# Gate weights gathered into one 36-column block; the first attention scores issued masks first, even and odd heads in turn

## The reference, cut to what matters

```
h = rmsnorm(x, norm1_g[l]);  proj = h @ w_in[l]
mq, mk, mv, mo, mi, mf, aq, ak, av, su = split(proj)
# (1) mi, mf: the input and forget gates of the mLSTM, 4 heads each, 8 columns of w_in in all
# (2) softmax attention, 8 heads of 64 features, 256 tokens, one block, causal:
s_own = einsum('bhqd,bhkd->bhqk', q, k) * scale
s_own = where(kpos <= qpos, s_own, -inf);  p = softmax(s_own)
```

## Time and profile before

| | us |
|---|---|
| median of three runs | 1274.5 |
| lowest, highest | 1273.63, 1278.43 |
| the profiled execution, its own time | 1275.59 |
| its span on the core | 1273.8 |
| TensorE busy (matmuls) | 1070.6 |
| VectorE busy | 460.3 |
| ScalarE busy | 180.1 |
| GpSimd busy | 22.4 |
| mean granted TensorE clock | 0.922 of 2.4 GHz |

### The profile page before, as it was taken

The page is one execution under the profiler, slowest core; times in us unless marked ns, Lnnn a source line. Parts: engine busy times, 40 slices in busy tenths (PEclk is TensorE's granted clock), DMA queues, the critical chain, the costliest instruction groups (busy, mean ns, idle before and its releaser), DMA issues.

```text
span 1273.8 us, 22730 instructions
## 1 busy us (share of the span) xinstructions
PE 1070.6 (84%) x9476; PEld 578.6 (45%) x9476; DVE 460.3 (36%) x1253; ACT 180.1 (14%) x427; POOL 22.4 (2%) x34
## 2 busy tenths in 40 slices
PE   5999999999967777776799999899677777679977
PEld 4476655454533333333355755554333333334533
DVE  0786345433322222222247753533222222224331
ACT  2314310010100000000024161100000000000100
POOL 3000002000000000000000000000000000000000
PEclk9999999999988888888899999999888888889998
DMA  9711379999999999999993313899999999997996
GB/s 313 261 71 67 132 291 355 389 428 426 430 427 427 425 428 429 427 427 427 391 339 141 133 67 132 353 387 428 427 427 427 426 428 427 428 427 327 427 426 278
DMA packets 50660, 440.16 MB, mean 346 GB/s; under 512 B 9320, under 2 KB 12040, under 8 KB 25488
## 3 DMA queue, kind: packets, MB, share of 16 engines
q1 hardware_dynamic: 48672, 436.33, 83.1%
q0 software_dynamic: 800, 0.99, 0.5%
q10 hardware_dynamic: 1104, 1.59, 0.4%
HBM read 437.31 MB, written 1.05 MB: 344 GB/s over the span
## 4 chain that ended last, share of the span: by engine, by line
PE 55%; DMA 40%; DVE 2%; issue 1%; DVEq 1%; ACT 0%; ACTq 0%; SPq 0%
DMA ring<-in_e_w_up_dram 39%; PE PS L1468 12%; PE PS L1531 9%; PE PS L1505 7%; PE PS L1767 4%; PE PS L1430 4%; PE PS L1421 4%; PE PS L1525 3%; PE PS L1440 2%; PE PS L1701 1%; PE PS L1721 1%; PE PS L1481 1%; DMA gT<-in_norm_g_dram 1%; PE PS L1657 1%; PE PS L1824 1%
## 5 line engine op out<-in xcount | busy, mean ns | idle before, releaser
L1468 PE MATMUL PS<-ring,hT 128*32 128x256 f32 x4608 | 336.6, 452 | 164.1 <-DMA ring<-in_e_w_gate_dram 107.7
L1468 PEld LDWEIGHTS PS<-ring,hT 128*32 128x32 f32 x4608 | 181.8, 125 | 339.6 <-issue 275.9
L1505 PE MATMUL PS<-ring,hT 128*32 128x512 f32 x1152 | 134.2, 607 | 8.5 <-issue 8.2
L880 DVE TENSOR_SCALAR hT<-hT 128x256 f32<-128x256 f32 x36 | 11.0, 306 | 302.4 <-ACT hT L613 302.4
L1531 PE MATMUL PS<-ring,hT 128*128 128x512 f32 x256 | 114.8, 602 | 0.0
L1430 PE MATMUL PS<-cst,ring 64*64 64x64 f32 x1216 | 81.2, 282 | 5.8 <-ACT ring L608 1.4
L1430 PEld LDWEIGHTS PS<-cst,ring 64*64 64x64 f32 x1216 | 77.0, 212 | 15.1 <-issue 11.9
L887 DVE TENSOR_TENSOR hT<-hT,PS 128x256 f32<-128x256 f32 x36 | 15.2, 422 | 174.7 <-PE PS L1468 174.7
L1421 PE MATMUL PS<-xres,scr 128*64 128x512 f32 x304 | 73.6, 605 | 0.0
L1531 PEld LDWEIGHTS PS<-ring,hT 128*128 128x128 f32 x256 | 48.1, 193 | 54.7 <-issue 54.6
L608 ACT COPY ring<-PS 128x512 f32<-128x512 f32 x38 | 22.3, 587 | 352.6 <-PE PS L1421 352.6
(11 more groups left out here) (341 smaller groups left out, 901.9 us busy)
## 6 DMA issues: line engine op xcount, KB each, us to landing
ring<-in_e_w_gate_dram SPq DMA_DIRECT2D x64, 2048.0 KB, 41.2
ring<-in_e_w_up_dram SPq DMA_DIRECT2D x64, 2048.0 KB, 44.0
ring<-in_e_w_down_dram SPq DMA_DIRECT2D x60, 2048.0 KB, 42.7
ring<-in_w_in_dram SPq DMA_DIRECT2D x10, 2048.0 KB, 18.8
ring<-in_w_out_dram SPq DMA_DIRECT2D x2, 4096.0 KB, 13.1
ring<-in_e_w_down_dram SPq DMA_DIRECT2D x8, 1024.0 KB, 39.5
ring<-in_w_in_dram SPq DMA_DIRECT2D x2, 1024.0 KB, 23.3
xres<-in_x_dram ACTq DMA_DIRECT2D x1, 1024.0 KB, 8.7
```

The lines of the kernel that those rows point to most:

```text
L1468: last = pe.matmul(PS[o:o + UT, bank, 0:256], xTe[:, k, UT * u:UT * u + UT], w[u][:, k, :, 2 * h:2 * h + 2], start=k == 0, stop=k == KD - 1)
L1505: last = pe.matmul(PS[o:o + UT, 3, :], hTe[:, c % 2, hc:hc + UT], w[u][:, c, 512 * h:512 * h + 512], start=c == 0, stop=c == KF - 1)
```

## The change

It has two parts. Part one: GpSimd waits for chunk 0 of `w_in`, clears a new block `wgates` of 8 x 36 columns (in tile 8 behind the chunk), and copies the eight gate columns into it, four to columns 0 to 3 and four to columns 32 to 35; TensorE waits for that (`s_wg`) and makes the gates with one matmul of 36 weight columns per feature block. The clearing of `v65`, `bb` and `taps` stands behind this in GpSimd's list. Part two: the first row tile's scores are issued differently. First two bf16 matmuls write the masks of four heads each, over a whole bank; then the eight fp32 matmuls of heads 0 to 7 add to them, even and odd heads in turn.

```diff
+        wgates = tile(8, KD * 264, KD * (32 + MH)).rearrange("p (k n) -> p k n", k=KD)
...
+                pool.wait_ge(s_win[0], 32 * (l + 1))
+                pool.memset(wgates, 0.0)
+                pool.drain()
+                for g in range(2):
+                    last = pool.tensor_copy(wgates[:, :, 32 * g:32 * g + MH], wchunk(0)[:, :, 256 + MH * g:256 + MH * g + MH])
+                last.then_inc(s_wg, 1)
                 pool.memset(v65[:, :, :, HD], 1.0).then_inc(s_zr, 1)
...
+                pe.wait_ge(s_wg, l + 1)
                 for k in range(KD):
-                    for g in range(2):
-                        last = pe.matmul(PS[32 * g:32 * g + MH, 1, 0:T], wchunk(0)[:, k, 256 + MH * g:256 + MH * g + MH],
-                                         hT[:, k, :], start=k == 0, stop=k == KD - 1)
+                    last = pe.matmul(PS[0:32 + MH, 1, 0:T], wgates[:, k, :], hT[:, k, :], start=k == 0, stop=k == KD - 1)
...
-                    if u >= 2:
-                        pe.wait_ge(s_pr, 6 * l + (u - 1))
-                    else:
-                        pe.wait_ge(s_qT, 4 * l + 4)
+                    pe.wait_ge(s_pr, 6 * l + (u - 1))
...
-                scores(0)
-                scores(1)
+                def first_scores():
+
+                    pe.wait_ge(s_qT, 4 * l + 4)
+                    for u in range(2):
+                        pe.matmul(PS[:, 6 + u, :].rearrange("p (i k) -> p i k", k=P), one16,
+                                  mask.unsqueeze(1).broadcast_to([P, 4, P]), start=True, stop=False)
+                    for h in range(AH):
+                        r = slice(64 * (h % 2), 64 * (h % 2) + 64)
+                        last = pe.matmul(PS[:, 6 + h % 2, P * (h // 2):P * (h // 2) + P], qkT[r, 0, h // 2, 0:P],
+                                         qkT[r, 1, h // 2, 0:P], start=False, stop=h >= AH - 2)
+                        if h >= AH - 2:
+                            last.then_inc(s_as, 1)
+
+                first_scores()
                 vo_part(0)
```

More of the change, by code:

```diff
@@ L220, in build @@
         s_wo = sem("w_out_in")
+        s_wg = sem("gate_columns_spread")
         s_tile = [sem(f"expert_tile_in_{t}") for t in range(NTILE)]
```

## The result

The changed kernel takes 1284.24 us, the median of 20 runs (1278.91 to 1289.72); the kernel before takes 1276.41 us beside it (20 runs). The ratio is 1.0055, with a 95% interval of 1.004 to 1.0069: slower by 7 us by the ratio, by 7.8 us between the two medians. I had forecast 1275.5 (1272 to 1280).

A forecast was written before the change was run, and what follows sets the result against it. TensorE's list was first suspect in the mixers, with VectorE the other parent at turn_probs(0). 1275.6 less 1.25 (1.07 scores, 0.18 gates) gives 1274.3; one clock fall (1.64) 1276.0, less 0.5 for the base: 1275.5 us, range 1272 to 1280.

The forecast's parts named there:

- The scores' work: First row tile's scores in each layer: 1.6 us (1.4 to 2.9) instead of 4.66, 3.1 us off TensorE's list.
- the 0.20 us read off the 128- and the 256-token records: Score matmuls of the heads: a fixed part of 0.20 us, paid once for a run of matmuls, not for each.
- the overlap read off L1440: Score matmuls over the two partition halves run together, so the eight heads take 1.04 us, not 1.88.
- Where the gain is cashed in: At turn_probs(0), which also waits for VectorE's L1191: gain 1.07 us in layer 0, 0 in layer 1.
- The clock, the step that failed: Idle time ahead of turn_probs(0) may halve TensorE's granted clock: 1.64 us a fall, 6 in 10 for each layer.
- two falls: Rival: the clock falls ahead of turn_probs(0) in both layers, 1277.6 us, slower by 2 us; 31 in 100.
- The gates: Gate matmuls in each layer: eight of 36 columns take 3.46 us instead of 3.55, gain 0.09 us a layer.
- GpSimd's work meets nobody: GpSimd's added clearing and copies for the gates, 0.7 to 2.4 us, delay no other engine; cost nothing.

The follow-up runs named there:

- e1: The kernel before with only the gates' part (gate columns spread by GpSimd, 36-column matmuls): 1276.77 us, ratio 1.0001.
- e10: The kernel before, unchanged, run once more for its trace: 1277.23 us, one execution.
- e3: The changed kernel with four matmuls that compute nothing needed between vo_part(0) and turn_probs(0): 1277.72 us, ratio 1.000.
- e2: The kernel before with only the scores' part (masks first, even and odd heads in turn): 1283.70 us, ratio 1.0054.
- e7: The changed kernel with GpSimd's three clears put back ahead of the gate columns: 1281.88 us, one execution.
- e9: The changed kernel, unchanged, run once more for its trace: 1288.62 us, one execution.
- e8: The kernel before with the scores' part only, vo_part(1) moved ahead of turn_probs(0) and vo_part(2) behind scores(2): 1268.31 us, ratio 0.9914.
- the first move alone: The changed kernel with vo_part(1) moved from behind scores(2) to ahead of turn_probs(0): 1277.61 us, ratio 1.0009.
- e5: The changed kernel with vo_part(1) moved ahead of turn_probs(0) and vo_part(2) behind scores(2): 1268.29 us, ratio 0.9931.

## Why the prediction was wrong

The chain of reasons was right in its order: the list gets shorter, VectorE is waited for, the clock falls. Its last link, what a fall costs, was mis-sized.

**The scores' work.** Forecast 1.6 us, measured 1.63: the masks 0.54 (0.53 forecast), the heads 1.09 (1.04 forecast). The first records of an even and an odd head start 7 ns apart, and the fixed part is paid once for the run. The two steps that carried it, the 0.20 us read off the 128- and the 256-token records and the overlap read off L1440, hold.

**Where the gain is cashed in.** Right for layer 0. L1199 ends at 107.48, `turn_probs(0)` starts 0.14 later, TensorE has been idle for 3.46 us (3.6 forecast). VectorE's last convolution input starts at 96.48 before (L1119) and at 96.07 after (L1127); from there to `turn_probs(0)` it is 11.55 us instead of 12.62: the 1.07 us forecast for layer 0. For layer 1 I forecast no gain, from the one layer of six in which the clock had held at the old scores; in e1 and e10 TensorE was 1.02 and 1.06 us late there too. The gain was under-read by up to 1 us, which makes the miss larger, not smaller.

**The clock, the step that failed.** I priced a fall at 1.64 us, the loss over the eight records of `vo_part(0)`, and gave it 6 in 10 in each layer. Both sizes were wrong. The chance was eight of eight. And the half clock is longer than the 3.4 us behind my 1.64: at the old scores it lasts 3.4 us in all five cases, behind the new wait 3.4 to 10.2, with 6.7 us of it over work on average. Half of that is lost, 3.4 us a layer, twice my price. The times say the same: filling the wait (e3) moves the ratio from 1.0055 to 1.000, 7 us or 3.5 a layer. Forecast for two layers was a loss of 2 x 0.6 x 1.64 = 2.0 us against a gain of 1.25. With the measured sizes it is a loss of 6.7 and 0.5 (GpSimd, below) against a gain of 1.7 (the average of the three traces before), so 5.5 us slower. Measured were 7.0, with an interval of 5.1 to 8.8, and 7.8 between the medians; 1.5 to 2.3 us are left over.

My price came from one fall, over `vo_part(0)` of layer 0 in one trace. Even with two falls the forecast gave 1277.6. The rows of the experts showed that the clock may fall within an idle time, but I did not ask how long it stays down behind one.

The profiled execution lost more than this, 6.74 and 7.65 us in its 60 us stretches. The rest of that are falls further down. They are not shown to be the wait's: the traces of e2 and e7, with the same wait, have 64.19 to 67.64 us there, while e1 and e3, without any, reach 65.78 and 66.87.

The Trainium skill (TensorE: Matmul & The Clock Gate, the section on HAM oscillation) tells of a kernel whose waits put TensorE back to half clock at every step of a loop. The eight waits of 3.5 us in four traces agree, and with that rule 6 in 10 was too low. It prices such a fall at half of the time spent throttled. The runs agree with that too: half of 6.7 us is 3.4 us a layer, and e3 gave back 3.5.

**The gates.** Forecast was a gain of 0.09 us a layer, measured is none (3.57 against 3.55). The term is small: eight matmuls of 36 columns take 0.446 us each, not 0.432; why they do not reach the full-width row is not shown.

**GpSimd.** Its copies cost 0.36 us for two, 0.3 each had been taken, and `s_wg` was up at 18.2 us (16.9 to 18.6 forecast). But "GpSimd's work meets nobody" was wrong. I had looked at VectorE's idle time in layer 0 and not at where the clears land in layer 1, behind 1.8 us of new work in GpSimd's list: on a VectorE copy that TensorE waits for. The term taken at nothing is 0.5 us, and 1.7 us more in the one trace of seven in which the clock fell behind it.

**What stays open.** That the unfilled wait causes the main part of the loss is shown (e3). Whether it also makes the clock fall more often later on, up to 53 us behind it, is not. In the changed kernel and in e9 layer 0 has two more stretches of half clock of 6.8 us each, in e2 none; e3, without any idle time, has two in layer 1, of 3.4 and 6.8 us (0.92), and e1 three there, of 3.4 each (0.92). One trace per run is too few for a rule.

## What to carry to other kernels

When work is taken from an engine that has a second parent shortly ahead, price the idle time that it leaves, not only the time that it fails to win: here 3.5 us of waiting in each layer cost about as much again behind the wait. Take the length of a half clock from several falls, behind waits like the new one, and not from a single row. Put needed dense work into the gap before judging the saving; the packed scores alone made the kernel slower by 0.54% (e2), and with two dense parts moved it is faster by 0.86% (e8), while the first move alone only found the next wait. And when work is put at the head of an engine's list, look in every layer at what its tail now runs beside.

## What the runs showed of the hardware

- Four matmuls that compute nothing, put in place of a wait in each of two layers, won about 7 us of 1284 (ratio 1.0055 to 1.000).
- The granted clock fell at eight of eight waits of 3.5 us, within the wait or less than 2 us behind it, and stayed at 1.2 GHz for 3.4 to 10.2 us. Where the old scores brought it down without any wait (five of six layers) it was back after 3.4 us.
- With the granted clock known, TensorE's time is additive: in the nine traces of the table that have all of the work in the stretch, 18 stretches of 61.5 to 70.7 us, length times granted clock is 60.3 to 61.6 us, and 57.5 to 58.3 in the two (e5, e8) with less work in it.
- A VectorE copy from one on-chip buffer to another, 8 x 128 in fp32, took 1.60 us instead of 0.20 while GpSimd cleared 2048 and 1024 columns, and ended 0.06 us after the clears. VectorE's product of PSUM with an on-chip operand just ahead of it (L851) ran beside the same clears at its usual 0.7 us (two in 1.52 us, before and after). The Trainium skill (GPSIMD Engine Reference, Specifications) says that GpSimd shares its interfaces to the on-chip memory with VectorE, and that they contend for some kinds of VectorE instructions; the trace agrees, one kind was delayed and the other was not. The copy ends with the last clear, which looks like an instruction held rather than slowed.
